# Paged key and value loads of a decoder step: a cache page laid over 32 partitions, four tokens in each

## The reference, cut to what matters

```python
past_k = pool_k[page_table].reshape(b, PAST_LEN, B_HEADS, 2, HEAD_DIM)
past_v = pool_v[page_table].reshape(b, PAST_LEN, B_HEADS, B_VDIM)
k_all = jnp.concatenate([past_k, bk.astype(past_k.dtype)], axis=1)
v_all = jnp.concatenate([past_v, bv.astype(past_v.dtype)], axis=1)
b_out = diff_head_norm(diff_attention_rows(bq, pos, k_all, v_all, lam), subln_g, lam_init)
```

## Time and profile before

| what | value |
|---|---|
| median of three executions | 1439.05 us |
| profiled execution, its time | 1440.42 us |
| profiled execution, its span | 1438.7 us |
| TensorE busy | 1375.7 us (96%) |
| VectorE busy | 936.2 us (65%) |
| ScalarE busy | 557.4 us (39%) |
| moved by DMA | 257.75 MB |
| attention stage | about 653 to 968 us of the span |

### The profile page before, as it was taken

The page is one execution under the profiler, slowest core; times in us unless marked ns, Lnnn a source line. Parts: engine busy times, 40 slices in busy tenths (PEclk is TensorE's granted clock), DMA queues, the critical chain, the costliest instruction groups (busy, mean ns, idle before and its releaser), DMA issues.

```text
span 1438.7 us, 27731 instructions
## 1 busy us (share of the span) xinstructions
PE 1375.7 (96%) x10683; PEld 1164.9 (81%) x10683; DVE 936.2 (65%) x1685; ACT 557.4 (39%) x1104; POOL 243.8 (17%) x272
## 2 busy tenths in 40 slices
PE   4999999999999999998999999989999999999997
PEld 4788988899998878885666666667899988999986
DVE  2222483489965656545566665657899974899848
ACT  4322343144542422125454554443554431345520
POOL 1000220155500000002111011000055500455200
PEclk8999999999999999999999999999999999999999
DMA  9998263133333143357899999993123324333431
GB/s 312 373 376 297 74 195 114 39 109 89 96 118 110 28 135 106 119 186 241 284 347 390 345 382 339 380 353 104 52 74 89 111 81 134 94 89 94 127 117 66
DMA packets 183021, 257.75 MB, mean 179 GB/s; under 512 B 11419, under 2 KB 103329, under 8 KB 182890
## 3 DMA queue, kind: packets, MB, share of 16 engines
q1 hardware_dynamic: 182890, 255.97, 53.0%
HBM read 248.05 MB, written 7.88 MB: 178 GB/s over the span
## 4 chain that ended last, share of the span: by engine, by line
PE 77%; DVE 10%; DMA 4%; issue 3%; SPq 3%; ACT 2%; POOL 1%; DVEq 0%; ACTq 0%; POOLq 0%
PE ps L1242 20%; PE ps L596 19%; PE ps L1887 8%; PE ps L340 6%; PE ps L2301 6%; PE ps L2313 3%; PE ps L600 3%; DVE ring_lo L1234 3%; PE ps L2369 3%; PE ps L1630 2%; DMA wada<-in_w_ada_dram 1%; SPq L2214 1%; PE ps L1874 1%; PE ps L2402 1%; DMA ring_raw<-in_ffn_w_in_dram 1%
## 5 line engine op out<-in xcount | busy, mean ns | idle before, releaser
L1234 DVE TENSOR_TENSOR ring_lo<-ring_raw,ring_hi 128x512 fp32r<-128x512 f32 x293 | 263.4, 932 | 65.9 <-ACT ring_hi L1222 63.8
L1222 ACT ACTIVATE ring_hi<-ring_raw 128x512 fp32r<-128x512 f32 x326 | 187.9, 620 | 163.1 <-DMA ring_raw<-in_ffn_w_out_dram 94.3
L596 PE MATMUL ps<-ring_hi,f 128*128 128x512 f32 x704 | 217.0, 389 | 0.0
L1242 PE MATMUL ps<-hhi,ring_hi 128*128 128x288 f32 x588 | 175.4, 298 | 6.3 <-DVE tmp L1449 3.0
L1242 PE MATMUL ps<-hlo,ring_hi 128*128 128x288 f32 x588 | 173.7, 295 | 0.0
L596 PEld LDWEIGHTS ps<-ring_hi,f 128*128 128x128 f32 x704 | 131.8, 188 | 27.0
L596 PE MATMUL ps<-ring_lo,f 128*128 128x512 f32 x352 | 137.0, 389 | 0.0
L1242 PE MATMUL ps<-hhi,ring_lo 128*128 128x288 f32 x456 | 134.8, 296 | 0.0
L2301 PEld LDWEIGHTS ps<-ident,k_ring 128*128 128x128 f32 x832 | 89.1, 141 | 55.7 <-issue 36.5
L2301 PE MATMUL ps<-ident,k_ring 128*128 128x128 f32 x832 | 121.0, 281 | 4.4 <-ACT KC L2526 3.0
L2614 DVE COPY KC<-ps 128x512 f32<-128x512 f32 (+2 forms) x128 | 75.3, 588 | 74.4 <-PE ps L2301 74.2
(11 more groups left out here) (301 smaller groups left out, 2884.1 us busy)
## 6 DMA issues: line engine op xcount, KB each, us to landing
wada<-in_w_ada_dram SPq DMA_DIRECT2D x18, 2048.0 KB, 14.1
ring_raw<-in_ffn_w_in_dram SPq DMA_DIRECT2D x140, 256.0 KB, 3.0
k_ring<-in_cache_diff_k_dram SPq DMA_DIRECT2D x128, 256.0 KB, 4.9
ring_raw<-in_ffn_w_out_dram SPq DMA_DIRECT2D x88, 256.0 KB, 3.5
v_rest<-in_cache_diff_v_dram SPq DMA_DIRECT2D x72, 256.0 KB, 4.8
k_ring<-in_cache_win_k_dram SPq DMA_DIRECT2D x16, 768.0 KB, 6.6
w<-in_w_qkv_dram SPq DMA_DIRECT2D x21, 512.0 KB, 3.8
w<-in_ffn_w_in_dram SPq DMA_DIRECT2D x18, 512.0 KB, 8.7
```

What stands on the lines that cost most here:

```text
L596: m = nc.tensor.matmul(ps[:, bank, :], x, w, start=(first and n == 0), stop=(last and n == 2), skip_group_check=True)
L1222: eng.activation(hi_of(g, i)[:], raw_of(g, i)[:], ACT.Copy).then_inc(sem("g_hi"), 1)
L1234: eng.tensor_tensor(lo_of(g, i)[:], raw_of(g, i)[:], hi_of(g, i)[:].bitcast(F32), ALU.subtract).then_inc(sem("g_lo"), 1)
L1242: m = nc.tensor.matmul(ps[:, bank, 0:TH], w, x, start=(first and n == 0), stop=(last and n == 2), skip_group_check=True)
```

## The change

For 16 or 17 of the 32 paged chunks (17 by its description; working the condition of `spread` through for all steps gives 16: five in each of the units 1, 3 and 5, and one in unit 7) a page is no longer put into one tile with a token to each of 128 partitions. It goes to 32 partitions, four consecutive tokens to each: page k of the chunk to partitions 32k to 32k+31, over the chunk's four tiles. The four tiles of a slot row lie side by side in a partition, so that a partition's four tokens are 8 KB in one piece both in the cache and in SBUF. A chunk is chosen where its four tiles are contiguous in both rings. Keys and values of a chunk change alike, and no compute instruction, wait or semaphore count changes. The number of transfers and their bytes stay the same.

```diff
+        def spread(u, s, c):
+
+            n = next(k for k in range(STEPS) if key_step(k) == (u, 1, s, c))
+            v = next(k for k in range(STEPS) if value_step(k) == (u, 1, s, c))
+            r = tiles_before(value_step, v) % RING
+            whole = r + 4 <= VFIRST or VFIRST <= r <= RING - 4
+            return v < APART_FROM and whole and key_tile(n, 0) <= RING - 4
...
+            def spread_page(is_v, seq, c, k):
+                rows = pool[is_v][ds(numbers[seq, c][k], 1), :, :]
+                return rows.rearrange("a (i j) c -> (a i) j c", j=4)
...
                     for k in range(4):
-                        eng.dma_start(k_ring[:, key_tile(n, k), :], page(0, seq, c, k)).then_inc(landed, 16)
+                        if spread(u, s, c):
+                            r = key_tile(n, 0)
+                            eng.dma_start(k_ring[32 * k:32 * k + 32, r:r + 4, :], spread_page(0, seq, c, k)).then_inc(landed, 16)
+                        else:
+                            eng.dma_start(k_ring[:, key_tile(n, k), :], page(0, seq, c, k)).then_inc(landed, 16)
...
                     for k in range(4):
-                        eng.dma_start(value_tile(v, k), page(1, seq, c, k)).then_inc(landed, 16)
+                        if spread(u, s, c):
+                            r = tiles_before(value_step, v) % RING
+                            region, r = (v_first, r) if r < VFIRST else (v_rest, r - VFIRST)
+                            eng.dma_start(region[32 * k:32 * k + 32, r:r + 4, :], spread_page(1, seq, c, k)).then_inc(landed, 16)
+                        else:
+                            eng.dma_start(value_tile(v, k), page(1, seq, c, k)).then_inc(landed, 16)
```

## The result

The changed kernel takes 1530.46 us (median of four, 1524.03 to 1548.78) against 1438.15 us before: ratio 1.0621, 95% interval 1.0597 to 1.0645. It is slower, as forecast, but by 92 us and not by 17, and lies outside the range. The execution of 1548.78 us was in a slower state and is left out of the ratio, by which the loss is 89 us. The profiled execution has a span of 1524.0 us, 85.3 us more than before.

A forecast was written before the change was run, and what follows sets the result against it. TensorE was taken to bound the attention stage, DMA close behind. Units 3 and 5 (12.8 us), unit 1 (2 us) and unit 7 (2.4 us) summed to +17 us, forecast 1456 us; range for 8 in 10 1434 to 1486 us.

The forecast's parts named there:

- What bounds the kernel: Attention stage: TensorE sets the pace at 75 us a pair of units, with the DMA engines close behind at 69.2 us.
- The mechanism: Changed page loads: each reaches 32 partitions, half of SBUF, so packets take f times as long, f between 1.0 and 2.
- The sum: Changed units: 12.8 us for units 3 and 5, 2 for unit 1, 2.4 for unit 7, together 17 us.
- The room: Pair of units in the attention stage: DMA needs 69.2 us of 75.0 at its best rate, leaving 5.8 us free.
- 14.4 us in the first: Unit 1's loads, stretch 665:745 at share 0.82: 14.4 us of room against 12.2 us needed; 2 us added.
- The neighbours: Unchanged loads queued beside changed ones in the attention stage: the forecast's sum has no term for them.
- The factor: Slowing of a changed 8 KB packet: f = 1.67 on 295 ns, a chunk 3.94 us, 1.22 us more than before.
- The upper end of the range: Attention stage with f = 2: +38 us, 1477; with most of the 5.8 us room unusable, +50 us, 1489.
- Hidden anyway: Attention stage: f 1.3 or less, a pair's 3.5 us fits the 5.8 us room; 1437 to 1445 us, chance 0.25.
- Faster: End of attention stage: 8 KB pieces at f = 1 leave less backlog, 7.5 us come back, 1431.5 us; chance 0.12.
- Pieces cut again: Changed pages: pieces may be cut into 2 KB again, +12 to +15 us in all, 1470 us; chance 0.08.
- TensorE's clock: Mid-stage: idle waits might drop the clock from 2.4 to 1.2 GHz, some us more; unpriced, no chance given.

The follow-up runs named there:

- the two lightened kernels: Kernel before with half the columns of value pages below step 58 left out, 1434.82 us; the same plus half of all paged key loads, 1434.44 us.
- both pairs of runs: Pages on 32 adjacent partitions (changed kernel, 1530.46 us) against every fourth, 1441.61 us; on 64 adjacent, 1527.13 us, against every second, 1440.62 us.
- three chunks: Only one chunk in each of units 1, 3 and 5 changed, against the kernel before: 1455.24 us, ratio 1.0111.
- the kernel with lighter values: Kernel before, value pages below step 58 loaded in half their columns: 1434.82 us; with one changed chunk in each of units 1, 3 and 5: 1445.24 us.
- the lightest kernel: Kernel before, half the columns left out of all paged key loads and of value loads below step 58: 1434.44 us, ratio 0.997.
- the lightened kernel: One changed chunk in each of units 1, 3 and 5, on the kernel with paged keys and values below step 58 halved: 1435.14 us, ratio 0.9966.
- ten loads in a unit: Only unit 3's five chunks changed, keys and values, against the kernel before: 1475.64 us, ratio 1.0255.
- five (15 us): Only unit 3's five key chunks changed, against the kernel before: 1453.45 us; only its five value chunks: 1453.11 us.

## Why the prediction was wrong

**What bounds the kernel.** Right: TensorE before, as the two lightened kernels show, with DMA close behind. Also right that after the change TensorE waits for `k_ring`, `v_rest` and `v_first`.

**The mechanism.** Right, and nearly the whole of the loss hangs on it: a transfer that reaches one half of the partitions runs at about half rate. Placement alone takes the cost from 6.2% to 0.2% (32 rows four apart, 64 rows two apart), and neither the size of the piece nor the number of partitions changes it. The rule of the Trainium skill in "SBUF — State Buffer", section on the DMA port swizzle, agrees, also in that partitions 0..63 are no better than 0..31; here 1527 us with 64 and 1530 with 32. The word of its section "Can I just issue two DMAs to hit both halves?", that two transfers to different halves serialize and gain 6%, is borne out too: alternating them made the packets 6% shorter (543 for 575 ns) and gave back a fifth of the loss.

One rival stays untested. In both pairs of runs the rows were spaced out in the same step that took them to both halves; no run spaces them within one half, or lays adjacent rows across the middle. Two things speak for the halves. Pages of 128 adjacent partitions run at the full rate, and alternating halves gained 20 us while each page's rows stayed adjacent.

**The size.** This is what failed. The sum took off room that wasn't there, gave the neighbours nothing without a reason, and had the factor too low. In the DMA engines' time over the stage:

1. *The room* (the step "DMA has 5.8 us of room in a pair", and 14.4 us in the first). This was the largest conceptual error. I compared a pair's mean rate with the best long stretch and called the difference free. At a share of 0.98 to 1.00 there was none: three chunks, 16 us of packet time, cost 16 us. In the first pair 23 us were paid too. Its 0.82 was read from the stretch 665:745, which starts 21 us before the pair; from mark to mark the share was 0.92. And in the changed kernel two of unit 1's five changed value chunks were asked for after 745 us. In the kernel with lighter values, at a share of 0.87 in 745:820, three chunks still cost 10 us. It takes the lightest kernel, at 0.78, to hide them. In the sum the room took off 12.2 + 11.6 us, less the 2 added: 22 us.
2. *The neighbours*, which had no term at all. Unchanged packets went from 92 to 98 ns (2 KB), 174 to 221 (4 KB) and 257 to 292 (6 KB): (18278 x 6 + 3647 x 47 + 3456 x 35) / 16 = 25 us.
3. *The factor.* I took 1.67 on 295 ns, 493 ns a packet. The mean was 575, so f = 1.95 on my 295 ns; on 309 ns, the median of an 8 KB packet that reaches both halves, it is 1.86. Either is near the upper end, where the engines work side by side. The changed pages took 4096 x 575 / 16 = 147 us where 16384 packets of 92 ns took 94: 53 us more, against 32 x 1.22 = 39 in the sum. 14 us. The factor alone is worth more, 4096 x 82 / 16 = 21 us; 7 us of it are offset because the packets replaced took 92 ns each and not my 85.

17 + 22 + 25 + 14 = 78 us, which is the 78 us of the packet sums. This is a count of engine time; that each us of it was paid in the span is read from the run with three chunks. The span grew by 85; the other 7 are engine time that went unused in the stage (405 - 380 = 25 us after, 320 - 302 = 18 before), as TensorE and the queue wait for each other in turn. The upper end of the range held f = 2 and no usable room in the full pairs, but room in the first, and nothing for the neighbours.

**The rivals.** *Hidden anyway* needs room and is what happened in the lightened kernel. *Faster* had the wrong sign of two things: nothing came back at the end of the stage (the load of `mix_raw` is 11.54 us of the chain, after 11.61), and a kernel with 31 us less of packet time gains only 4. *Pieces cut again* is out by the packet count. *TensorE's clock* I left without a price. It was at half for some 58 us of the stage after, and none before. TensorE's busy time over the whole execution grew from 1375.7 to 1394.3 us, so longer matmuls make at most about 19 of the 85 us, as busy time goes. How much of that counts is open, since no run held the clock up while TensorE waited.

**Open.** Why the kernel before has no usable room at 366 GB/s when it can run at 397. Its 2 KB packets took 92 ns on average and 84 in the median; what lengthens them wasn't tried. Also why the price of ten loads in a unit (36 us) is more than twice that of five (15 us), and what part the clock has in it.

No version was faster than before. With both halves reached, the larger pieces are neither gain nor loss that matters (+0.18%, +0.22%), since TensorE sets the pace.

## What to carry to other kernels

Look at which partitions one transfer reaches before looking at the size of its pieces: 32 or 64 adjacent partitions ran at half rate whatever the pieces, and the same rows spaced over all 128 ran at nearly the full one. A half-rate transfer in a shared queue also costs its neighbours; here they made up about a third of the added packet time. And read the room from the share, not from the rate. At a share of 0.98 to 1.00 added packet time was paid in full here, though TensorE set the pace and the mean rate was below that of the best stretch; at 0.78 it was hidden.

## What the runs showed of the hardware that was not expected

- The engines of one queue seem to stay together (a reading of the packet times, not shown directly): with the lone store as the only evidence I had allowed for engines a packet or two apart, but the mean factor over 4,096 packets was 1.95, and alternating halves brought it only to 543 / 295 = 1.84.
- A transfer of 128 partitions is slowed by a half-rate one beside it: 353 ns for a 4 KB packet in one stretch, more than double, and 312 ns on average beside four or more changed packets, against 174 ns beside none.
- A strided placement of the 32 rows has a median packet of 309 ns and a mean of 370: 13% of the packets took over 450 ns. What lengthens these was not tried.
